# The last four output tiles of a hybrid attention layer: tile 14 scaled on ScalarE and multiplied on GpSimd, bias passes of tiles 13 and 14 moved behind tile 15's statistics

## The reference, cut to what matters

```
h = x @ w_in                                   # one projection: q, k, v and gates of both mixers, merge gates
ya = (windowed_sink_attention(...) * silu(za)) @ w_proj_a
yb = (blockwise_global_attention(...) * silu(zb)) @ w_proj_b
y  = (sigmoid(ga + b) * ya + sigmoid(gb + b) * yb) @ w_out
out = layer_norm(DN_ALPHA * x + y, ln_g, ln_b)   # over 1024 columns, float32
```

## Time and profile before

| | us |
|---|---|
| three runs | 665.65, 664.14, 759.37 |
| their median | 665.65 |
| the profiled execution, its own time | 664.49 |
| its span on the slowest core (core 7) | 662.8 |
| the spans of all eight cores | 660.6 to 662.8 |

### The profile page before, as it was taken

How to read it: one execution, slowest core, us unless ns; L and a number is a source line. 1 busy time by engine, 2 the same in 40 slices (tenths; PEclk the granted TensorE clock), 3 DMA queues, 4 the chain that set the end, 5 groups by cost and what they waited for, 6 DMA issues and landing times.

```text
span 662.8 us, 13686 instructions; the slowest of 8 cores (660.6 to 662.8 us)
## 1 busy us (share of the span) xinstructions
PE 606.9 (92%) x4440; PEld 233.0 (35%) x4440; DVE 374.1 (56%) x740; ACT 390.7 (59%) x515; POOL 127.1 (19%) x193
## 2 busy tenths in 40 slices
PE   2889988998799999999999999999999999999990
PEld 0356632333233333333333333333333333344440
DVE  3198752234546353546774855366668445498467
ACT  0155678876686667565756576756776677721220
POOL 2268634011001011110131111011211110114022
PEclk9899999999899999999999999999999999999996
DMA  8987809955005444431465624345662423336303
GB/s 124 135 155 107 124 2 173 146 74 116 4 1 97 64 64 65 65 44 22 96 126 98 129 50 89 55 65 96 126 193 65 101 45 49 65 118 142 58 1 128
DMA packets 26773, 57.61 MB, mean 87 GB/s; under 512 B 3024, under 2 KB 5200, under 8 KB 26448
## 3 DMA queue, kind: packets, MB, share of 16 engines
q0 software_dynamic: 21520, 39.36, 39.7%
q1 hardware_dynamic: 5184, 17.38, 7.5%
HBM read 86.65 MB, written 8.39 MB: 143 GB/s over the span
## 4 chain that ended last, share of the span: by engine, by line
PE 78%; DVE 7%; issue 5%; ACT 5%; DMA 3%; POOL 1%; DVEq 0%; ACTq 0%; POOLq 0%
PE PS L257 77%; ACT PT L266 3%; DMA SZ<-ws 2%; DMA XT<-xT 1%; DVE G L272 1%; DVE O L269 1%; ACT G L266 1%; PE PS L405 1%; DVE D L835 1%; DVE T L269 1%; DVE STT L579 0%; DVE SZ L272 0%; DVE QB L272 0%; DVE QA L272 0%; DVE R L840 0%
## 5 line engine op out<-in xcount | busy, mean ns | idle before, releaser
L266 ACT ACTIVATE PT<-PS 128x1024 bf16<-128x1024 f32 (+1 forms) x304 | 293.5, 1017 | 109.3 <-PE PS L257 108.4
L257 PE MATMUL PS<-XT,WROT 128*128 128x512 bf16 x896 | 220.0, 381 | 3.6 <-DVE G L272 3.5
L257 PEld LDWEIGHTS PS<-XT,WROT 128*128 128x128 bf16 x896 | 77.2, 98 | 116.8 <-issue 42.6
L276 POOL DMA_DIRECT2D WROT<-wg x100 | 53.4, 536 | 296.2 <-PE PS L257 295.2
L257 PE MATMUL PS<-PT,VX 128*64 128x512 bf16 (+3 forms) x688 | 99.3, 366 | 10.3 <-DVE O L269 7.6
L257 PE MATMUL PS<-QB,KB 64*128 64x512 bf16 x512 | 80.8, 383 | 5.9 <-ACT PT L266 5.4
L272 DVE SCALAR_TENSOR_TENSOR G<-G,PS 128x512 f32<-128x512 f32 x64 | 43.1, 683 | 73.9 <-PE PS L257 64.2
L266 ACT ACTIVATE G<-PS,CVH 128x512 f32<-128x512 f32 x64 | 44.1, 688 | 64.8 <-PE PS L257 64.8
L257 PE MATMUL PS<-SZ,XT 128*128 128x384 bf16 (+1 forms) x256 | 57.5, 370 | 16.1 <-DMA XT<-xT 15.8
L257 PE MATMUL PS<-SZ,WR 128*128 128x512 bf16 x256 | 63.9, 380 | 1.5 <-ACT G L266 1.2
L257 PE MATMUL PS<-WR,T 128*128 128x512 bf16 x256 | 60.8, 380 | 0.2 <-DVE T L269 0.2
(11 more groups left out here) (68 smaller groups left out, 439.1 us busy)
## 6 DMA issues: line engine op xcount, KB each, us to landing
WROT<-wg POOLq DMA_DIRECT2D x100, 256.0 KB, 7.2
T<-x SPq DMA_DIRECT2D x8, 512.0 KB, 6.7
out<-T SPq DMA_DIRECT2D x8, 512.0 KB, 3.8
QB<-x SPq DMA_DIRECT2D x6, 512.0 KB, 6.5
out<-QB SPq DMA_DIRECT2D x6, 512.0 KB, 3.1
SZ<-ws POOLq DMA_DIRECT2D x8, 256.0 KB, 9.2
XT<-xT POOLq DMA_DIRECT2D x2, 1024.0 KB, 10.5
WR<-wo POOLq DMA_DIRECT2D x8, 256.0 KB, 19.1
```

The lines of the kernel that those rows point to most:

```text
L257: s.op("pe", lambda e: e.matmul(out, lhsT=lhsT, rhs=rhs, start=start, stop=stop, skip_group_check=skip), reads=reads, writes=writes)
L266: s.op("act", lambda e: e.activation(out=out, in_=in_, func=func, **kw), reads=reads, writes=writes)
L276: s.op(eng, lambda e: e.dma_start(out=out, in_=in_), reads=reads, writes=writes, dma=True)
```

## The change

- `stats()`: the nmr is made for every tile above 11, so tile 14 gets one. The `norm` of tiles 12, 13 and 14 is called at once, inside `stats()`, and no longer by the next tick. Only tiles up to 11 go through `jobs`.
- Tile 12: as before, `scale`, mul, and `later(4, shift)`; but `now` is one lower when this is called.
- Tile 13: `scale` and mul as before; its `shift` goes to a new list `ends`.
- Tile 14: `gain` and `back` on VectorE go away. `scale` (ScalarE) takes their place, and its mul (GpSimd) and its `shift` (VectorE, and the send) go to `ends`.
- Tile 15: behind its statistics come the `shift` of 13 and the mul of 14, then its own passes and sends as before, and last the `shift` of 14 with its send.

```diff
@@ stats()
-                if t in (12, 13, 15):
+                if t > 11:
                     s.op("dve", lambda e: e.tensor_scalar(out=SM[:, st, 2:3], ...
-                if t < 15:
+                if t < 12:
                     jobs.append(norm)
                 else:
-                    while jobs:
+                    while t == 15 and jobs:
                         jobs.pop(0)()
                     norm()
@@ norm()
-                if t in (12, 13):
+                if t < 12:
+                    gain(0, 2)
+                    jobs.append(store)
+                elif t < 14:
                     scale(0, 2)
                     affine("pool", LNG, ("LNG",), ALU.mult, 0, 2)
-                    later(4, shift)
-                elif t < 15:
-                    gain(0, 2)
-                    jobs.append(store)
+                    if t == 12:
+                        later(4, shift)
+                    else:
+                        ends.append(shift)
+                elif t == 14:
+                    scale(0, 2)
+                    ends.append(lambda: affine("pool", LNG, ("LNG",), ALU.mult, 0, 2))
+                    ends.append(shift)
                 else:
+                    ends.pop(0)()
+                    ends.pop(0)()
                     gain(0, 1)
                     scale(1, 2)
                     back(0, 1)
...
                     affine("dve", LNB, ("LNB",), ALU.add, 1, 2)
                     send(1, 2)
+                    ends.pop(0)()
```

More of the change, by code:

```diff
@@ L534, in build_program @@
         jobs = []
+        ends = []
         quiet = [False]
```

## The result

The changed kernel takes 670.51 us (median of 4 runs, 670.17 to 670.86) against 665.46 before: ratio 1.0075, with a 95% interval of 1.0062 to 1.0087, so about 5.0 us more (4.1 to 5.8). The forecast was 669.6.

The account below looks back on a forecast made before the run. It took VectorE's queue to set the end: -0.1 + 1.14 (shift of 13) + 2.0 (hold) + 1.14 (shift of 14) + 0.8 (larger last send) = +5.0 us, giving 669.6, range 666.5 to 672.0.

Parts of the forecast that it names:

- the main case: Last 20 us: early shift of 12 waits, shift of 13 held by the mul of 14; +5.0 us, 669.6; chance 0.66.
- The order of the shift of 12: VectorE queue at tile 13: shift of 12 moves ahead of tile 13's second half, a new wait of 2.5 us.
- C: Tile 13: tick count off by one, shift of 12 stays behind tile 13's statistics; +2.3, 666.8; chance 0.07.
- The sum up to tile 15's nmr, -0.1: VectorE queue before tile 15's nmr: 3.74 us removed, waits for GpSimd put about 3.65 back.
- The hold: Behind tile 15's nmr: GpSimd's mul of 14 holds VectorE's shift of 13, both reading two SBUF operands; +2.0 us.
- Rival B: Behind tile 15's nmr: mul and VectorE run side by side, shift of 13 takes 1.22; +3.0, 667.5; chance 0.10.
- D: VectorE queue, 641.6 to 657: tile 14's freed time is kept, GpSimd truly parallel; +0.2, 664.7; chance 0.03.
- The last send: End of span: last send 512 KB instead of 256, landing in 2.6 to 2.9 against 2.0; +0.8 us.
- rival E: Tail: sends pile up or the mul grows under VectorE's passes; +6 to +7.5, 670.5 to 672; chance 0.14.

## Why the prediction was right

The measured time lies 0.9 us above the forecast, within its range, and the main case held in each of its steps. The span came out at 669.1 and not 667.8: 1.6 us of that difference arose upstream of tile 12's pow, which the forecast took as unchanged, and the terms themselves were 0.2 us too large.

**The order of the shift of 12.** Counted from the values of `now`, one tick earlier, ahead of the second half of tile 13. The trace shows it there, with an idle of 2.49 us (forecast 2.5), and the run that moved it back gave 2.6 us back. C is refuted.

**The sum up to tile 15's nmr, -0.1.** Measured -0.07. What tile 14's removed passes and the moved shift of 13 freed on VectorE, 3.74 us, was given back by two waits for GpSimd: the one for the mul of 12 (2.5, of which 2.4 are left at tile 14's statistics), and the round trip of tile 14's new nmr behind the mul of 13 (1.3). The steps were right one by one: the second STT of tile 13 came 5.96 behind tile 12's pow (forecast 645.22 - 639.27 = 5.95), tile 15's nmr 17.87 (forecast 17.85).

**The hold.** Forecast 2.0, in a pass shown with 3.2 us or so; measured 3.15 - 1.22 = 1.93. Rival B (side by side) is refuted by the run with the short mul, and the run with the PSUM operand shows which passes are concerned. That the two engines share the time in parts is refuted as well: the mul kept its 2.34, and the shift ended 1.08 after it, so that all but 0.14 of its 1.22 was done after the mul. No run varied what GpSimd reads or writes. By the rule of the Trainium skill's page SBUF — State Buffer, section SBUF: two separate sides, the first of the two engines keeps the shared port pair for its whole instruction; the trace agrees over 2.07 us of a mul that was begun 0.27 us before the shift. It agrees as well with the page's condition that a VectorE operation outside the two-port modes is concerned when it has two SBUF inputs. D needed what B and C assume and fell with them; even with both costs taken out by hand, the change ends at 1.0009. (The terms given for D add up to +0.3 and not +0.2, which changes nothing.)

**The last send.** Forecast +0.8 from landings, measured +0.56 from the last pass to the end of the span. This is the one term that was mis-sized in the stretch, by 0.2 us. It was worked out from 2.6 to 2.9 against 2.0, and the last send landed at the lower end, 2.6. The median of 670.51 touches the lower end of rival E, but neither of its causes is in the trace: the mul of 14 kept its 2.34, and the pile of sends did no harm in the changed kernel, whose last send is issued 1.1 us behind the one before.

**From the stretch to the median.** The stretch costs 4.7 us and the medians differ by 5.0. The rest lies within the interval of the ratio, and what makes it stays open.

## What to carry to other kernels

When one engine's queue sets the end, count for every pass taken out of it the waits that the substitute puts in: a 128x1 step that goes to another engine and back costs 0.8 to 1.0 us of idle time, and an addition that follows a long GpSimd pass has to stand behind something else to do. A callback that is due a number of ticks after its call moves when the call moves, even inside an edit meant for another tile. GpSimd passes over SBUF belong beside VectorE passes that read PSUM or a single SBUF operand; the conflict showed as a longer duration and not as a wait, so compare durations of the same form. Before you divide a last send, look at what the program waits for behind it, and in which order.

## What the runs showed of the hardware that I had not expected

- A GpSimd instruction that is held got in between two VectorE passes that stand directly one behind the other, even where the second is shown as begun before the first has ended (648.39 against 648.47). A short pow did no harm there (a pair of gains kept 1.41 us); a mul of 2.35 held the second pass to its end (3.36 for 1.28).
- Each wait of SP for a semaphore that has already arrived took 0.05 us. Ten of them behind the last landing made 0.5 us (0.8 in place of 0.3 from that landing to the end of the span).
- Three sends of 256 KB issued 0.55 and 0.65 us apart kept the DMA engines full at 385 GB/s, and the last landed 2.2 to 2.6 us after its issue, not 2.0.
